# The bias tables of group B, loaded through ScalarE's DMA queue instead of SyncE's

## The reference: what is computed

```
rpb_c = rpb[:, :, dc_idx]                       # rpb: heads x 15 x 31
bias = rpb_c[:, dr_idx].transpose(0, 2, 1, 3)
sc = einsum('bqhd,bikhd->bhqik', q_row, k_strip) * scale + bias[None]
sc = where(col_ok, sc, -inf);  p = softmax(sc);  out = p @ v_strip
```

## Time and profile before

| | |
|---|---|
| time, median of 3 runs | 2101.56 us (2097.13 to 2101.99) |
| profiled execution | 2096.63 us |
| its span, first to last instruction | 2094.8 us |
| TensorE busy | 2035.8 us, 97% of the span |
| VectorE, ScalarE, GpSimd busy | 62%, 39%, 23% |
| mean granted TensorE clock | 0.988 of full |
| DMA, all queues | 212.64 MB, of which q10 (ScalarE's) 1.13 MB |

### The profile page before, as it was taken

One profiled execution on the slowest core, in us unless ns is written; L12 is line 12 of the kernel. 1 busy time (PEld: TensorE's weight loads), 2 busy tenths in 40 slices (PEclk: granted clock), 3 DMA queues, 4 the chain that ended last, 5 costly groups with the idle time before them and its releaser, 6 DMA issues.

```text
span 2094.8 us, 28973 instructions
## 1 busy us (share of the span) xinstructions
PE 2035.8 (97%) x9990; PEld 1626.6 (78%) x9990; DVE 1304.2 (62%) x1761; ACT 822.5 (39%) x1361; POOL 485.7 (23%) x339
## 2 busy tenths in 40 slices
PE   7999999999989999999999999999999999999996
PEld 6788886565567788788888888888888888787885
DVE  6799735888767855886665566556643544334546
ACT  6323213444466811363444344434433433423223
POOL 4122204666621234111122112211200100102101
PEclk9999999999999999999999999999999999999998
DMA  5132456311189341212211221122156444341103
GB/s 185 71 141 106 180 155 177 62 45 45 43 161 174 64 179 61 91 36 66 70 53 58 65 70 53 57 65 70 50 205 235 173 150 150 120 140 40 41 31 121
DMA packets 82688, 212.64 MB, mean 102 GB/s; under 512 B 26560, under 2 KB 26944, under 8 KB 82624
## 3 DMA queue, kind: packets, MB, share of 16 engines
q1 hardware_dynamic: 81760, 210.70, 32.8%
q10 hardware_dynamic: 864, 1.13, 0.1%
HBM read 156.75 MB, written 55.05 MB: 101 GB/s over the span
## 4 chain that ended last, share of the span: by engine, by line
PE 79%; DVE 8%; issue 5%; ACT 2%; DMA 2%; POOL 1%; SPq 1%; DVEq 0%; ACTq 0%; POOLq 0%
PE ps L326 23%; PE ps L327 23%; PE ps L328 23%; PE ps L1270 2%; DVE qstd L742 1%; PE ps L1216 1%; DMA TR<-in_rpb 1%; PE ps L1224 1%; DVE qt L755 1%; PE ps L1201 1%; POOL key_sum L1126 1%; PE ps L1304 1%; SPq L1041 1%; PE ps L1280 1%; PE ps L1188 1%
## 5 line engine op out<-in xcount | busy, mean ns | idle before, releaser
L326 PE MATMUL ps<-NH,WH 128*128 128x512 f32 x840 | 333.8, 397 | 18.3 <-DVE WL L725 9.5
L327 PE MATMUL ps<-NL,WH 128*128 128x512 f32 x840 | 330.3, 393 | 0.0
L328 PE MATMUL ps<-NH,WL 128*128 128x512 f32 x840 | 330.0, 393 | 0.0
L326 PE MATMUL ps<-NL,NH 128*128 128x512 f32 x528 | 207.0, 392 | 3.6 <-ACT tok_std L1608 3.5
L327 PE MATMUL ps<-NH 128*128 128x512 f32 x528 | 206.4, 391 | 0.0
L328 PE MATMUL ps<-NL 128*128 128x512 f32 x528 | 206.2, 391 | 0.0
L327 PE MATMUL ps<-NL,AH 128*128 128x512 f32 x528 | 205.7, 390 | 0.0
L326 PE MATMUL ps<-NH,AH 128*128 128x512 f32 x528 | 205.7, 390 | 0.0
L328 PE MATMUL ps<-NH,AL 128*128 128x512 f32 x528 | 205.7, 390 | 0.0
L2455 DVE TENSOR_TENSOR NL<-raw,NH 128x1024 fp32r<-128x1024 f32 x66 | 81.9, 1241 | 197.4 <-ACT NH L2309 197.4
L326 PEld LDWEIGHTS ps<-NH,WH 128*128 128x128 f32 x840 | 159.7, 190 | 56.6 <-DVE NL L719 10.6
(11 more groups left out here) (253 smaller groups left out, 4067.3 us busy)
## 6 DMA issues: line engine op xcount, KB each, us to landing
raw<-in_w SPq DMA_DIRECT2D x102, 512.0 KB, 3.4
A_raw<-in_wu SPq DMA_DIRECT2D x84, 256.0 KB, 2.6
act<-ca SPq DMA_DIRECT2D x22, 768.0 KB, 3.3
NH<-act SPq DMA_DIRECT2D x66, 256.0 KB, 3.5
xst<-in_xT SPq DMA_DIRECT2D x24, 256.0 KB, 3.7
H<-in_xT SPq DMA_DIRECT2D x8, 768.0 KB, 8.9
H<-hT SPq DMA_DIRECT2D x8, 768.0 KB, 6.5
out_yT<-H SPq DMA_DIRECT2D x24, 256.0 KB, 2.1
```

The lines of the kernel that those rows point to most:

```text
L326: nc.tensor.matmul(out, wh, xh, start=first, stop=False, skip_group_check=onto)
L327: nc.tensor.matmul(out, wh, xl, start=False, stop=False, skip_group_check=onto)
L328: return nc.tensor.matmul(out, wl, xh, start=False, stop=last, skip_group_check=onto)
```

## The change

Tables (i + 1, 0) and (i + 1, 1), for pairs 1 to 3, are no longer loaded by SyncE. ScalarE loads them within pair i: after its other work of step 5 and of step 15 it waits for `tab[1 - s]`, adds one to a semaphore of its own, and issues the same eight DMAs on its own queue. The tables of pair 0 stay with SyncE. The addresses are made by `table_rows`, a new function that both use. SyncE's loop issues queries and keys alone.

```diff
--- before.py
+++ after.py
@@ -851,7 +851,7 @@
         q_ld, k_ld = ({kind: [sem(f"{x}{kind}{s}") for s in range(2)] for kind in "AB"} for x in ("q_ld", "k_ld"))
         v_ld = {kind: sem(f"v_ld{kind}") for kind in "AB"}
         all_stored = sem("all_stored")
-        zeroed, pe_passed, dve_passed, sp_passed = (sem(x) for x in ("zeroed", "pe_passed", "dve_passed", "sp_passed"))
+        zeroed, pe_passed, dve_passed, sp_passed, act_passed = (sem(x) for x in ("zeroed", "pe_passed", "dve_passed", "sp_passed", "act_passed"))
         s_rdy, m_done, e_done = sem("s_rdy"), sem("m_done"), sem("e_done")
 
         t_rdy, t_free = ([sem(f"{x}{b}") for b in range(2)] for x in ("t_rdy", "t_free"))
@@ -1028,17 +1028,19 @@
             step("B", NPAIR, None, 1, "B", None)
             step("B", NPAIR, None, 2, "B", None)
 
+        def table_rows(i, s):
+            row = RPB_PADDED[1]
+            for r in range(NA_ROWS):
+                yield TR[cols(r, NA_COLS), :, :], bass.AP(tensor=a["rpb_tensor"], offset=(i * 2 + s) * (RPB_PADDED[0] * row) + row * r,
+                                                          ap=[[1, NA_COLS], [row, TAB_ROWS], [1, TAB_COLS]])
+
         def s2_sync(sp):
             def load_table(i, s):
-                if not isinstance(i, int) or i or s:
+                if i or s:
                     sp.wait_ge(tab[1 - s], i + s)
                     sp.sem_inc(sp_passed, 1)
-                row = RPB_PADDED[1]
-                for r in range(NA_ROWS):
-
-                    src = bass.AP(tensor=a["rpb_tensor"], offset=(i * 2 + s) * (RPB_PADDED[0] * row) + row * r,
-                                  ap=[[1, NA_COLS], [row, TAB_ROWS], [1, TAB_COLS]])
-                    nc.sync.dma_start(TR[cols(r, NA_COLS), :, :], src).then_inc(t_ld[s], 16)
+                for dst, src in table_rows(i, s):
+                    nc.sync.dma_start(dst, src).then_inc(t_ld[s], 16)
 
             def scored(p, s):
 
@@ -1080,7 +1082,6 @@
                     sp.sem_inc(sp_passed, 1)
                     load_queries("B", i, s)
                     load_keys("B", i, s)
-                    load_table(i, s)
 
         def s2_presets(pool):
             for s, count in ((o_done, O_FREE), (o_acc, ACC_FREE_O), (t_free[0], T_FREE), (t_free[1], T_FREE), (v_free, V_FREE),
@@ -1373,6 +1374,12 @@
                 _, w = window(kind, m)
                 act.wait_ge(t_rdy[b], fills(kind, p, ("T", m)))
                 nc.scalar.activation(turned_dst_b(m, w), turned_src(b, len(key_blocks(w))), ACT.Copy).then_inc(t_free[b], 1)
+
+            def load_table(i, s):
+                act.wait_ge(tab[1 - s], i + s)
+                act.sem_inc(act_passed, 1)
+                for dst, src in table_rows(i, s):
+                    nc.scalar.dma_start(dst, src).then_inc(t_ld[s], 16)
 
             def spread_copy(p, b):
 
@@ -1424,6 +1431,8 @@
                     square(p - 1, 1)
                 if m == 3:
                     square(p - 1, 2)
+                if after == "B" and m in (5, 15):
+                    load_table(i + 1, m // 15)
                 if m == 20:
                     square(p, 0)
                 if m == 23:
```

## The result

The changed kernel takes 2129.31 us (median of 4 runs, 2128.05 to 2129.38), the kernel before 2099.56 (median of 4, 2097.13 to 2101.99): 1.0149 times the time before, 95% interval 1.0135 to 1.0163. That is 30 us slower, where 20 were forecast; 2129.3 lies in the range of 2107 to 2136. The profiled executions are 2129.38 and 2096.63 us, with spans of 2127.6 and 2094.8.

What follows compares the result with a forecast made beforehand. Steps within a pair were taken as bound by TensorE, with ScalarE's lead being spent. Terms -4.9 + 11.1 + 9.9 + 3.9 = +20.0 us gave 2116.6 from the profiled execution, 2121 from the shown median; range 2107 to 2136.

Steps and rivals of the forecast that it cites:

- gain at the changes of pair: Group B's three changes of pair: VectorE's waits for tables of s = 0 go, gaining 4.9 us.
- stalls of step 5: ScalarE's wait for GpSimd's table and eight issues delay the next exponential; TensorE loses 3.7 us three times, 11.1.
- stalls of step 15: ScalarE's eight issues, without a wait, delay the next exponential; TensorE loses 3.3 us three times, 9.9.
- clock: TensorE's granted clock falls after four of six stalls, 5.2 us, less the existing fall's 1.3: +3.9 us.
- second rival: Steps 5 and 15: the queue holds ScalarE's issues, +26 us (2147), or step 15 only, +13 (2134); 12%.
- Part 1: Changes of pair: tables of s = 0 are issued 7 us earlier, VectorE's three waits go; 4.9 us gained.
- Part 2: Steps 5 and 15: eight issues hold ScalarE 4.0 us, TensorE waits for the exponential; 21.0 us lost.
- Part 3: After the new stalls TensorE's clock falls four times, 1.3 us each, less one existing fall: 3.9 us lost.
- Part 4: SyncE loses 48 issues; queries and keys keep their margin, no cost; without it a table's 3.3 us would be late.
- first rival: Steps 5 and 15: issues are cheap on ScalarE, deciding at 0.19 us per DMA; near 0 the time is 2095.4; 7%.

Runs made afterwards that it cites:

- e2: The kernel before, with SyncE loading both tables ahead of queries and keys of the same s, ScalarE issuing nothing: 2090.10 us, ratio 0.9965.
- e6: e2 with the table of s = 1 issued by ScalarE in step 15, s = 0 still early on SyncE: 2107.52 us, ratio 1.0045 to the kernel before.
- e4: The changed kernel plus 32 useless transposes on TensorE in steps 8 and 18, before it waits for the late exponential: 2122.80 us, ratio 1.0126.
- e3: The changed kernel with ScalarE issuing one table DMA in each of steps 5 to 12 and 15 to 22: 2123.86 us, ratio 1.0131.
- e9: The changed kernel with the first table issued at the end of step 7 instead of step 5: 2131.53 us, ratio 1.0160.
- e5: The changed kernel with ScalarE issuing two table DMAs in each of steps 5 to 8 and 19 to 22: 2100.99 us, ratio 1.0010.
- e7: e2 plus eight DMAs of 16 numbers into an unused column, issued by ScalarE in steps 5 and 15: 2117.93 us, ratio 1.0090 to the kernel before.

## Why the prediction was right in kind and short in size

The mechanism held at each place: the waits for tables gone, eight issues under ScalarE, two stalls a pair, released by ScalarE. The size did not. The period of a pair was to be about 43 us and is 47.3 and 47.5 (first load of queries to the next). The terms against what the two profiled executions show:

| term | predicted | measured |
|---|---|---|
| gain at the changes of pair | -4.9 | -4.2 |
| stalls of step 5 | 3.7 x 3 = 11.1 | 5.82 + 4.51 + 4.45 = 14.8 |
| stalls of step 15 | 3.3 x 3 = 9.9 | 4.73 + 4.02 + 3.73 = 12.5 |
| clock | +3.9 | +10.6 |
| sum | +20.0 | +33.7 (32.8 in the span) |

That 2129.3 lies in the range is luck in part. The forecast was 2121, 8 us lower, and it stood on the shown median of 2101.56; from the profiled execution, where the terms were read, it was 2116.6, and that execution came out at 2129.38, 13 us higher. The upper end of 2136 took in half of the second rival, eight issues in step 15 that last 8.27 us like SyncE's; none here took over 5.6. And the upper bound of the clock term, 6.5, was passed by 4.

**Part 1** (the gain) was right, and e2 isolates it: 2.5, 1.8 and, from the last load of values on, 1.6 us, 5.9 in all with the old fall of the clock and less the 1.54 us of its wait for keys, where 4.9 + 1.3 were put down. (The working takes off 0.65 us where it says 0.75; that is 0.2 us in the sum.) The rule of the Trainium skill that was weighed against it ("DMA: Bandwidth & Descriptors", "Rules for kernel authors": spreading over issuing engines only saves issue time) would have made it 0. Here the tables landed in 2.5 us, not 9.5, and the waits went, so a gain of 0 was wrong; but e2 got as much from one queue by order alone, so the second queue was not needed for it, and the trace does not speak against the rule itself.

**Part 2** (the stalls) is the first term mis-sized: 27.3 us instead of 21.0. In the stall at 636 us ScalarE was held 4.48 us, not 4.0; GpSimd's table reached it 0.25 us later than it ended; from the last issue to the copy went 0.11 and from the exponential to TensorE 0.22. Of these hops only 0.2 us, for the wait and the increment, had been counted. And a step: "I expect no issue above a microsecond" was wrong, the longest is 1.62 us, beside SyncE's keys. e6 shows that this held part can grow to 6.74 us for seven issues. So the half of the second rival that was put at step 15 is real in kind, but at 0.6 to 1.6 us over the 4.0 (5.57 us of hold in pair 1, 4.87 and 4.58 in the others), not 4.3.

**Part 3** (the clock) is the term that failed most: four falls of 1.3 us, against six and 10.6 us. The price came from one short fall, the one in the earlier trace rows, and five of the six falls here last twice as long as that one: 3.4 us there, 6.8 here. The length of the stall doesn't tell which it is: the stall of 4.51 us had the short fall, the one of 3.73 a long one. e4 shows that the loss is the clock's: fill the stall, and a pair with more work is 4.4 us shorter.

**Part 4** (SyncE) was right in its cost: nothing waits for queries, keys or values. Its estimate of 3.3 us was not sound, since the 8.27 and the 4.94 us are of two different tables (the second took 8.87 us to issue), and it looked only at what a table does to the keys. What queries and keys do to a table on the other queue shows in e3 and e9. **The first rival** (an issue costs less than 0.19 us) was out by the issue rows and stays out: 0.32 to 0.35 us, and 0.48 to 0.52 from one to the next where nothing holds it.

One thing stays open: e5 and e2 differ by 11 us (9 by their ratios), of which the pairs' windows show 5.8 for one pair; how much of that a place later than step 5 for the first two issues would give back wasn't tried.

## What to carry to other kernels

A DMA issue cost its engine's stream a third to half a microsecond here, for 64 bytes and for 48 KB, and up to 1.6 us when it was held. Before moving issues onto a computing engine, measure how far that engine is ahead of its consumer, and keep each run of issues, with any wait in front of it, under that lead. If a transfer is late only since it stands behind others on its queue, first try to move it up in the same queue, and look at what then stands behind it. And price a stall of TensorE with the clock that follows, from more than one fall: the six here cost 10.6 us, on top of 27.3 us of stalls.

## What the hardware did that I had not expected

A small transfer on a quiet queue was not always fast beside a busy one. In e3 and e9 DMAs of 48 KB in pieces of 192 bytes took up to 12.4 and 14.1 us to land on ScalarE's queue while queries and keys moved on SyncE's; the quickest took 2.0 and 2.1. It depended on when: the tables of step 15 in the changed kernel, issued 9 us and more after the first queries, took 4.6 at most. By the Trainium skill ("DMA: Bandwidth & Descriptors", "Queues, rings and completion order") a DMA engine goes round its queues packet by packet; packets of such small pieces that alternate with packets of SyncE's pieces of 6 KB would look like this, but no run here separates that from other causes. And an issue that nothing holds hardly depends on the bytes: eight DMAs of 64 bytes took ScalarE 3.62 us at the least in e7, eight of 48 KB 3.82 in e9. In the changed kernel eight took 4.4 to 5.6.
